# Products of the modulation vectors as scaled copies on ScalarE, sums on GpSimd over 1024 columns

## The reference

```
silu_c = silu(c)
for l in range(2):
    mod_lat = silu_c @ ada_w[l] + ada_b[l]              # ada_w[l]: 1024 x 6144
    sh1, sc1, g1, sh2, sc2, g2 = split(mod_lat, 6)
    a_lat = rms_norm(x, mix_norm[l]) * (1 + sc1) + sh1
    y = even_mixer(a_lat, a_ctx, ...) if l == 0 else pool_mixer(a_lat, ...)
    x = x + g1 * y
    f = rms_norm(x, ffn_norm[l]) * (1 + sc2) + sh2
    gate, val = split(f @ w_up[l], 2)                   # w_up: 1024 x 5632
    gate = dwconv3(gate, conv_w) + conv_b
    x = x + g2 * ((silu(gate) * val) @ w_down[l])       # w_down: 2816 x 1024
```

## Time and profile before

| | us |
|---|---|
| median of 3 runs | 1250.97 |
| lowest, highest run | 1250.73, 1255.97 |
| span of the profiled execution | 1251.2 |

### The profile page before, as it was taken

The page is one execution under the profiler, slowest core; times in us unless marked ns, Lnnn a source line. Parts: engine busy times, 40 slices in busy tenths (PEclk is TensorE's granted clock), DMA queues, the critical chain, the costliest instruction groups (busy, mean ns, idle before and its releaser), DMA issues.

```text
span 1251.2 us, 13400 instructions
## 1 busy us (share of the span) xinstructions
PE 1076.4 (86%) x4684; PEld 852.4 (68%) x4684; DVE 748.0 (60%) x741; ACT 416.9 (33%) x534; POOL 485.2 (39%) x319
## 2 busy tenths in 40 slices
PE   5859779877976988999989987835999999999997
PEld 2349656665765766887767876723788888888876
DVE  1595776768586667536774476698544434443452
ACT  3432233333222543223231232333454223422332
POOL 0081563568465788608883289141100000000000
PEclk9888889999996999999999998966999999999999
DMA  8631232343344454525544344401232323342322
GB/s 289 229 101 64 85 101 92 94 133 89 110 139 118 119 149 154 182 68 164 154 151 143 110 129 131 127 1 34 67 101 100 102 80 89 100 126 76 92 76 68
DMA packets 152700, 141.87 MB, mean 113 GB/s; under 512 B 4738, under 2 KB 137432, under 8 KB 152664
## 3 DMA queue, kind: packets, MB, share of 16 engines
q1 hardware_dynamic: 140672, 99.27, 26.1%
q0 software_dynamic: 11520, 41.95, 11.2%
q10 hardware_dynamic: 472, 0.18, 0.1%
HBM read 139.28 MB, written 2.10 MB: 113 GB/s over the span
## 4 chain that ended last, share of the span: by engine, by line
PE 62%; DVE 22%; issue 5%; POOL 5%; ACT 4%; DMA 1%; ACTq 0%; DVEq 0%; POOLq 0%; SPq 0%
PE pair L526 18%; PE pair L527 18%; PE pair L528 18%; DVE w_lo L1089 5%; POOL acc L471 3%; DVE a_lo L1145 2%; POOL ada_raw L459 2%; DVE cb L1361 1%; PE pT L600 1%; DVE tmp L1135 1%; DVE tmp L1122 1%; DVE h_lo L1089 1%; PE pT L735 1%; DVE cb L1365 1%; DVE tmp L1288 1%
## 5 line engine op out<-in xcount | busy, mean ns | idle before, releaser
L526 PE MATMUL pair<-a_hi,w_hi 128*128 128x512 f32 x864 | 356.5, 413 | 80.8 <-DVE w_lo L1089 24.8
L527 PE MATMUL pair<-a_lo,w_hi 128*128 128x512 f32 x864 | 349.6, 405 | 0.0
L528 PE MATMUL pair<-a_hi,w_lo 128*128 128x512 f32 x864 | 348.5, 403 | 0.0
L1089 DVE TENSOR_TENSOR w_lo<-w_raw,w_hi 128x2048 fp32r<-128x2048 f32 (+1 forms) x119 | 232.1, 1957 | 48.1 <-ACT w_hi L813 35.2
L526 PEld LDWEIGHTS pair<-a_hi,w_hi 128*128 128x128 f32 x864 | 170.2, 197 | 128.3 <-issue 39.1
L471 POOL TENSOR_TENSOR acc<-acc,ada_raw 128x512 f32<-128x512 f32 x120 | 204.2, 1702 | 9.4
L528 PEld LDWEIGHTS pair<-a_hi,w_lo 128*128 128x128 f32 x864 | 170.0, 197 | 37.6
L527 PEld LDWEIGHTS pair<-a_lo,w_hi 128*128 128x128 f32 x864 | 170.5, 197 | 34.6 <-issue 0.5
L526 PE MATMUL pair<-h_hi,w_hi 128*128 128x512 f32 (+1 forms) x432 | 170.0, 394 | 14.1 <-DVE w_lo L1089 11.1
L813 ACT ACTIVATE w_hi<-w_raw 128x2048 fp32r<-128x2048 f32 x68 | 129.6, 1906 | 128.3 <-PE pair L528 128.3
L527 PE MATMUL pair<-h_lo,w_hi 128*128 128x512 f32 (+1 forms) x432 | 167.7, 388 | 0.0
(11 more groups left out here) (212 smaller groups left out, 1017.8 us busy)
## 6 DMA issues: line engine op xcount, KB each, us to landing
w_raw<-in_ffn_w_up_dram SPq DMA_DIRECT2D x88, 512.0 KB, 5.0
ada_raw<-in_ada_w_dram POOLq DMA_DIRECT2D x80, 512.0 KB, 4.1
w_raw<-in_ffn_w_down_dram SPq DMA_DIRECT2D x32, 512.0 KB, 4.4
w_raw<-in_even_w_in_dram SPq DMA_DIRECT2D x20, 512.0 KB, 4.6
w_raw<-in_ffn_w_down_dram SPq DMA_DIRECT2D x16, 384.0 KB, 3.9
w_raw<-in_ada_w_dram SPq DMA_DIRECT2D x10, 512.0 KB, 4.9
w_raw<-in_even_w_out_dram SPq DMA_DIRECT2D x8, 512.0 KB, 4.6
ada_raw<-in_ada_w_dram SPq DMA_DIRECT2D x6, 512.0 KB, 6.4
```

Of the source, the lines that this page charges most:

```text
L526: nc.tensor.matmul(dst, lh, rh, start=start, stop=False)
L527: nc.tensor.matmul(dst, lh, rl, start=False, stop=False)
L528: return nc.tensor.matmul(dst, ll, rh, start=False, stop=stop)
L1089: return nc.vector.tensor_tensor(dst, full, hi.bitcast(f32), ALU.subtract)
```

## The change

The product of a chunk moves from GpSimd to ScalarE (`ada_product`): two copies of 128 x 512, in place, each with a scale per partition from `silu_c`. GpSimd now adds whole chunks, 128 x 1024: chunk 0 + chunk 1 into `acc` (both halves of it), then + chunk 2, + chunk 3, and at last one sum of `acc`'s halves (128 x 512). Chunks 2 and 3 are both issued after the first of these sums. In `MIX` a unit `prod` for each of 36 chunks (9 blocks) stands every 2.8 steps from step 5 on, and the reductions are set at steps 20, 31, 42, 54, 65, 76, 87 and 98 (before: 16, 28, 44, 56, 68, 76, 92 and 110). In layer 0's up loops ScalarE makes the products of the block after the one that is reduced in the same pair: chunk 2u before the weight split of the slot, chunk 2u + 1 after it.

```diff
--- before.py
+++ after.py
@@ -90,7 +90,10 @@
             3: [("qf", 2), ("qf", 3)], 4: [("qf", 4)]},
         4: {1: [("st", 5)], 2: [("iv", 5)], 3: [("st", 6), ("rot", 5)], 4: [("iv", 6)], 5: [("qf", 5)],
             6: [("rot", 6)], 7: [("qf", 6)]}}
-    ada_steps = {(2, 0): 0, (3, 4): 1, (5, 4): 2, (7, 0): 3, (8, 4): 4, (9, 4): 5, (11, 4): 6, (13, 6): 7}
+    chunk_steps = {}
+    for ch in range(4 * (ADA0 + 1)):
+        chunk_steps[5 + 14 * ch // 5] = ch
+    ada_steps = {12 + 14 * (4 * b + 3) // 5: b for b in range(ADA0)}
     conv = {5: ("cvc", 0), 6: ("cvb", 0), 8: ("cvc", 1), 9: ("cvb", 1)}
     for n in range(OUT0 + 4):
         free = [k for k in range(8) if not any(u[0] == "sc" for u in attention.get(8 * (n - 3) + k, []))]
@@ -101,8 +104,10 @@
             s.extend(head_tiles.get(n, {}).get(k, []))
             if n - 1 in (5, 8) and k in (1, 2, 3, 4):
                 s.append(("tap", (n - 6) // 3, (k - 1) // 2, (k - 1) % 2))
-            if (n, k) in ada_steps:
-                s.append(("ada", ada_steps[n, k]))
+            if 8 * n + k in chunk_steps:
+                s.append(("prod", chunk_steps[8 * n + k]))
+            if 8 * n + k in ada_steps:
+                s.append(("ada", ada_steps[8 * n + k]))
             if n and k in split_steps:
                 s.append(("sp", n + 1, split_steps.index(k)))
         s.append(("ev", n))
@@ -111,6 +116,8 @@
     return s
 
 
+ADA0 = 8
+ADA1 = 12
 MIX = mixer_schedule()
 
 T_USE = {u: i for i, u in enumerate(u for u in MIX if u[0] in ("ada", "tr") or
@@ -125,8 +132,6 @@
 AUX_NORM = [1] + [3 + len(AUX_USE) + 2 * i for i in range(3)]
 SC_USE = {u: i for i, u in enumerate(u for u in MIX if u[0] == "sc")}
 ROTS = [u for u in MIX if u[0] == "rot"]
-ADA0 = 8
-ADA1 = 12
 
 
 
@@ -241,6 +246,7 @@
         aux_read = [sem(f"aux_read{i}") for i in range(3)]
         prod_done = sem("prod_done")
         acc_done = sem("acc_done")
+        half_sum = sem("half_sum")
         ada_ready = sem("ada_ready")
         ada_summed = sem("ada_summed")
         ada3_loaded, row_copied, ada_cols = sem("ada3_loaded"), sem("row_copied"), sem("ada_cols")
@@ -451,31 +457,26 @@
                 pool.dma_start(ada_raw[:, q % 2, :].rearrange("p (k n) -> p k n", k=2),
                                src[:, 2 * q:2 * q + 2, col_block, :]).then_inc(ada_loaded[q % 2], 16)
 
+            wide = acc[:, :, :].rearrange("p a t -> p (a t)")
+
             def ada_sum(b, src, col_block, next_src, next_block, first=False):
 
-                for q in range(4):
-                    w = ada_raw[:, q % 2, :].rearrange("p (k n) -> p k n", k=2)
-                    pool.wait_ge(ada_loaded[q % 2], 32 * b + 16 * (q // 2 + 1))
-                    nc.gpsimd.tensor_tensor(w, w, silu_c[:, 2 * q:2 * q + 2].unsqueeze(2).to_broadcast([P, 2, SEQ]),
-                                            ALU.mult).then_inc(prod_done, 1)
-                    pool.wait_ge(prod_done, 4 * b + q + 1)
-                    if q == 0:
-                        if first:
-                            pool.wait_ge(mods_done, 1)
-                        else:
-                            pool.wait_ge(ada_ready, b)
-                        nc.gpsimd.tensor_tensor(acc[:, 0, :], w[:, 0], w[:, 1], ALU.add).then_inc(acc_done, 1)
-                    else:
-                        for kk in range(2):
-                            pool.wait_ge(acc_done, 7 * b + 2 * q - 1 + kk)
-                            nc.gpsimd.tensor_tensor(acc[:, 0, :], acc[:, 0, :], w[:, kk], ALU.add)\
-                                .then_inc(acc_done, 1)
-                    if q < 2 or next_src is not None:
-                        pool.wait_ge(acc_done, 7 * b + 2 * q + 1)
-                        if q < 2:
-                            chunk(src, col_block, q + 2)
-                        else:
-                            chunk(next_src, next_block, q - 2)
+                pool.wait_ge(prod_done, 8 * b + 4)
+                if first:
+                    pool.wait_ge(mods_done, 1)
+                else:
+                    pool.wait_ge(ada_ready, b)
+                nc.gpsimd.tensor_tensor(wide, ada_raw[:, 0, :], ada_raw[:, 1, :], ALU.add).then_inc(half_sum, 1)
+                pool.wait_ge(half_sum, 3 * b + 1)
+                chunk(src, col_block, 2)
+                chunk(src, col_block, 3)
+                for q in (2, 3):
+                    pool.wait_ge(prod_done, 8 * b + 2 * q + 2)
+                    nc.gpsimd.tensor_tensor(wide, wide, ada_raw[:, q % 2, :], ALU.add).then_inc(half_sum, 1)
+                    pool.wait_ge(half_sum, 3 * b + q)
+                    if next_src is not None:
+                        chunk(next_src, next_block, q - 2)
+                nc.gpsimd.tensor_tensor(acc[:, 0, :], acc[:, 0, :], acc[:, 1, :], ALU.add).then_inc(acc_done, 1)
 
             def lo_by_pool(n):
                 pool.wait_ge(w_split, n)
@@ -671,7 +672,7 @@
 
             def ada_reduce(b, use):
 
-                pe.wait_ge(acc_done, 7 * b + 7)
+                pe.wait_ge(acc_done, b + 1)
                 if isinstance(use, int) and use == 0:
                     pe.wait_ge(mods_done, 1)
                 else:
@@ -825,6 +826,14 @@
                 nc.scalar.activation(w_hi[:, n % 2, part], w_raw[:, n % 2, part], ACT.Copy)\
                     .then_inc(w_hi_done if c == 3 else w_quarter, 1)
 
+            def ada_product(b, q):
+
+                act.wait_ge(ada_loaded[q % 2], 32 * b + 16 * (q // 2 + 1))
+                for kk in range(2):
+                    w = ada_raw[:, q % 2, kk * SEQ:(kk + 1) * SEQ]
+                    k = 2 * q + kk
+                    nc.scalar.activation(w, w, ACT.Copy, scale=silu_c[:, k:k + 1]).then_inc(prod_done, 1)
+
             def square(norm, k, final):
 
                 act.wait_ge(*final)
@@ -956,6 +965,8 @@
                     evac_in(unit[1])
                 elif kind == "sp":
                     hi_quarter(unit[1], unit[2])
+                elif kind == "prod":
+                    ada_product(unit[1] // 4, unit[1] % 4)
                 elif kind == "st":
                     act.wait_ge(*stat_ready(unit))
                     if unit[1]:
@@ -1034,7 +1045,11 @@
                             nc.scalar.activation(cb[:, v, :], cb[:, v, :], ACT.Silu).then_inc(g_ready, 1)
                             act.wait_ge(*bank_done(s, 1))
                             nc.scalar.activation(h_hi[:, 2 * i + u, :], cb[:, v, :], ACT.Copy).then_inc(hh_ready, 1)
+                            if l == 0:
+                                ada_product(ADA0 + 1 + j0 // 2 + i, 2 * u)
                             hi_of_slot(s)
+                            if l == 0:
+                                ada_product(ADA0 + 1 + j0 // 2 + i, 2 * u + 1)
                     pairs(act, nk // 2, up)
                     n0 += nk
                     final = part == 2
```

## The result

The changed kernel takes 1273.84 us (median of 4 runs, 1272.18 to 1276.06) against 1250.98 for the kernel before (4 runs on the same chip): a ratio of 1.0175 (95% interval 1.0147 to 1.0203). It is slower; I had given that 0.16, and the time is outside my range. The profiled execution has a span of 1270.6 us.

The account below looks back on a forecast made before the run. TensorE, busy 86% of the span, bounds the kernel, though in layer 0's up loops GpSimd's blocks hold it back. 1251.2 - 13 + 8 - 8 - 1 - 6.5 = 1230.7, predicted as 1231 us, range 1208 to 1256.

Parts of the forecast that it names:

- start, to slot 3: Before the first product GpSimd has no sums, so TensorE's first stage wait ends near 84 instead of 92.4: gain 8.
- attention, slot 3 to slot 10: Shorter VectorE instructions cut TensorE's waits, the third head loses, the fourth gains: gain 1 us in all.
- output projection: Late chunk 2 delays the weight split and `w_lo`; TensorE waits 7.9 us before slot 12, 2.9 before 13: loss 8.
- norm: Earlier eighth reduction, block 8 already summed, copy 1.8 us shorter, 4.7 from five other instructions held off: gain 6.5.
- layer 0's three loops: GpSimd stops setting the pace; pairs take 22.4 first, then about 25 us, with waits for `w_lo`: gain 13.
- product pairs fit in ScalarE's idle time, of which it has two thirds of the span: Attention: ScalarE's added products cost nothing there, part of the term that gains 1 us.
- the reading by share: Whole kernel: GpSimd's 39% busy share tells nothing; its effect must be sought stage by stage in TensorE's waits.
- the third head: Attention: chunk 2's product chains 9.3 us where 3 is covered, a loss of 5.5 with the clock.
- 5.5 us of TensorE's waits less: From slot 3 to the third head, VectorE's longest instructions get shorter, so TensorE waits 5.5 us less.
- the wait at the end of slot 2 keeps this gain: Start: `v_hi` waits for chunk 2 of block 1, but would have waited for VectorE; the gain of 8 stays.
- the wide sum alone: GpSimd's sum of 1024 columns, taken as 2.35 us from a line between 512 and 2048 columns; bounds 1.91 and 2.54.
- The rival of late chunks: Chunk 2 lands after 7.6 instead of 4.1 us, ScalarE waits ahead of the weight split: 1281 us, chance 0.16.

Follow-up runs that it names:

- quarter_first: Changed kernel, with the quarter of the next weight slot's w_hi ahead of the product of the same mixer step in ScalarE's order: 1248.80 us.
- wide_before: Kernel before, products kept on GpSimd, its seven sums of 512 columns replaced by three of 1024 and one of 512: 1264.84 us.
- the delay runs: Changed kernel and orders_paired, each wide sum replaced by two 64-column sums around a small transfer that GpSimd waits for: 1284.64 and 1225.46 us.
- Short products: Changed kernel, with ScalarE's products taken over 64 of the 512 columns of each half: 1236.73 us.
- up_split_first: Changed kernel, with ScalarE making the next slot's w_hi before both products in layer 0's up loops: 1246.82 us.
- orders_paired: Changed kernel with the order edits of quarter_first and up_split_first, mixer products in two pairs per block, and transposes at step 11: 1197.02 us.
- paired_late_reduce: orders_paired, but with TensorE's transposes of the finished sums at the changed kernel's steps, three to four later: 1221.50 us.

## Why the prediction was wrong

By its own terms (us, gains negative; up loops by the differences in the second fence, 116.0, 114.3 and 86.8):

| term | predicted | measured |
|---|---|---|
| start, to slot 3 | -8 | -3.1 (159.64 against 162.72) |
| attention, slot 3 to slot 10 | -1 | +26.5 |
| output projection | +8 | +9.1 (49.1 against 40.0) |
| norm | -6.5 | -9.8 (23.2 against 33.0) |
| layer 0's three loops | -13 | -1.4 |
| behind the last loop's second down slot | 0 | -1.9 |

**The step that failed** is "product pairs fit in ScalarE's idle time, of which it has two thirds of the span", by which the attention was to gain 1 us; it lost 26.5. That is the reading by share of which the prediction itself warned for GpSimd. An idle engine's queue is not a free one: in the attention ScalarE is idle because it waits for work that is about to come, and each of its instructions has somebody behind it. I followed the chain product, quarter, `w_lo` in the up loop and the output projection, where it came out, but in the attention I counted only the third head. There VectorE's order carries the delay on from a weight quarter, which has time, to a maximum, which has none. Order alone was worth 20.2 us at slot 10 (quarter_first).

Part of the 26.5 is TensorE's clock. In the windows from slot 3 to slot 10, before and after, the same stage has a mean granted clock of 0.94 and of 0.87, so more of it is at the lower of its two levels, 1.2 GHz, and TensorE is busy 139.1 and 150.4 us (columns: the window and its length, busy us of TensorE, its weight loads, VectorE, ScalarE and GpSimd, the granted clock, DMA share and GB/s):

```profile
162.00:332.00 170.00, 139.07 (x630) 107.67 (x630) 120.99 (x153) 57.25 (x106) 100.52 (x73) 0.94 0.34 103
```

```profile
159.00:356.00 197.00, 150.40 (x649) 117.84 (x648) 114.07 (x157) 82.46 (x146) 59.03 (x42) 0.87 0.30 92
```

Busy time times clock is 131 us in both, so it is the same work at a lower clock: 11 of the 27 us are slower matmuls and 16 are gaps. In the attention the prediction had a term for the clock only in the third head.

**Holding.** I summed how long GpSimd holds VectorE (16.5 us a block before, 8.3 after) and took the smaller sum for a gain: the "5.5 us of TensorE's waits less" of the attention. VectorE was indeed less busy, but a hold costs by when it comes. Before, GpSimd went from product to sum by itself; after, most sums that it waits for are released by ScalarE's product, as VectorE's next piece is by the quarter behind it. The size up to slot 10 is 12 us in wide_before, where only GpSimd's work changed, and at least 17.6 and 18.7 in the delay runs. These prices are from three kernels and are not to be added to the order's 20.2 us, a part of which is a hold avoided, as at the third exponential above.

**Layer 0's loops.** The mechanism was right: one wait of ScalarE for chunk 2 in each pair, 15.0 us in 11, 1.4 each where I had about 1, and TensorE waiting for `w_lo`. The size was not: pairs came at 22.3, 24.6, 26.5 and 26.7 us in the second loop, not 25, since sums that met a `w_lo` of 2048 columns took 3.27 us instead of 2.35 and the tap behind took 2.87. Short products and up_split_first both show what the order hid, 16 and 26 us.

**Start.** TensorE's wait ended at 80.93, earlier than my 84. But "the wait at the end of slot 2 keeps this gain" did not hold: ScalarE stood 8.2 us behind chunk 2 of block 1, until 136.9, with `v_hi` behind it, and TensorE waited 10.4 us for `v_lo` where it had waited 8.5.

**Right** were the output projection (TensorE waited 8.3 and 5.4 us for `w_lo` ahead of slots 12 and 13; I had 7.9 and 2.9), the norm in its direction (9.8 where I had 6.5), and the wide sum alone (2.34). The rival of late chunks gave the right side for a wrong reason. The landing of chunks after the change:

```profile
DMA to landing us min/median/max: 3.9/4.6/7.4
```

The median is 0.5 us above that of the earlier trace rows and the maximum no higher. By the Trainium skill, "SBUF — State Buffer", section "SBUF: two separate sides", VectorE could have kept GpSimd from writing the descriptors of these transfers; no run here shows it. In the mixer chunks were late because they were issued late, behind `acc`: with the transposes earlier (orders_paired against paired_late_reduce) 24.5 us go.

## What to carry to other kernels

Work moved to an idle engine costs first by its place in that engine's order (here 25 and 27 us) and only then by its length (17 us with the places right): for each insertion name what stands behind it, who waits for that, and what stands behind the waiter on its own engine. Put filler that may wait for a transfer behind the instruction that feeds another engine, and give the transfer its whole round (sum, issue, landing, and the reader that must free the buffer first) before the step that needs it; here such edits alone turned 1.8% slower into 4.4% faster. The time for which one engine holds another is not to be added up: ask what releases the long instruction, and what the engine that it holds has to do just then.

## What the runs showed of the hardware

- An add of 1024 f32 columns on GpSimd takes 2.34 us alone and 3.27 when it meets a VectorE subtraction of 2048 columns; a VectorE add of 4 columns took 1.7 to 2.2 us behind such a sum, and 0.16 without.
- A scaled copy of 64 columns on ScalarE takes 0.34 us on average, one of 512 columns 0.71.
- A transfer of 128x4 f32 issued by GpSimd was there 1.95 us after its issue began in the mixer (210.54 to 212.49), and GpSimd's waits for it were up to 5.1 us in layer 0's up loops, where the transfer engines were busy 44% of the time and not 30%.
